# Pairing the first two output chunks of a hybrid attention layer in seven block products, with weight sums made by accumulating transfers

## The reference

```python
h = rmsnorm(x, g_norm)
proj = jnp.einsum('bsd,de->bse', h, w_in)
...
y_moba = rmsnorm(o_moba * jax.nn.silu(m_z), g_out_moba)
...
y_nsa = rmsnorm(o_nsa * jax.nn.silu(n_z), g_out_nsa)
y = jnp.concatenate([y_moba, y_nsa], axis=-1)
return x + jnp.einsum('bse,ed->bsd', y, w_out)     # and then rmsnorm(x, g_final)
```

## Time and profile before

| what | value |
|---|---|
| median of 3 runs | 495.84 us (495.82 to 496.1) |
| the profiled execution | 495.77 us |
| its span, first to last instruction | 494.0 us |
| TensorE busy | 484.8 us (98%), 2502 matmuls |
| VectorE busy | 354.1 us (72%) |
| ScalarE busy | 261.7 us (53%) |
| GpSimd busy | 64.1 us (13%) |
| granted TensorE clock, mean | 0.996 |

### The profile page before, as it was taken

How to read it: one execution, slowest core, us unless ns; L and a number is a source line. 1 busy time by engine, 2 the same in 40 slices (tenths; PEclk the granted TensorE clock), 3 DMA queues, 4 the chain that set the end, 5 groups by cost and what they waited for, 6 DMA issues and landing times.

```text
span 494.0 us, 6523 instructions
## 1 busy us (share of the span) xinstructions
PE 484.8 (98%) x2502; PEld 402.4 (81%) x2502; DVE 354.1 (72%) x561; ACT 261.7 (53%) x374; POOL 64.1 (13%) x66
## 2 busy tenths in 40 slices
PE   8999999999999999999999999999999999999993
PEld 7887787877788888888888888888888888888882
DVE  5888855932699948776587887765888667888643
ACT  5886353642656535645544455664675664366422
POOL 2340100100112202000020200000332240040120
PEclk9999999999999999999999999999999999999998
DMA  8989894577576552543544724448247679433304
GB/s 292 325 287 385 302 330 148 195 251 260 136 268 194 171 171 85 171 130 127 171 142 157 255 63 156 140 151 303 85 148 300 239 266 361 167 139 121 135 0 170
DMA packets 56783, 97.50 MB, mean 197 GB/s; under 512 B 4560, under 2 KB 15408, under 8 KB 56368
## 3 DMA queue, kind: packets, MB, share of 16 engines
q1 hardware_dynamic: 54544, 96.03, 56.7%
q10 hardware_dynamic: 2208, 1.06, 0.9%
HBM read 93.93 MB, written 2.10 MB: 194 GB/s over the span
## 4 chain that ended last, share of the span: by engine, by line
PE 96%; issue 1%; DMA 1%; ACT 0%; DVE 0%; ACTq 0%; POOLq 0%; POOL 0%; SPq 0%; DVEq 0%
PE proj L692 26%; PE proj L694 26%; PE proj L693 26%; PE b_o L988 4%; PE b_t L673 2%; PE b_p L957 2%; PE proj L725 2%; PE b_s L858 2%; PE proj L731 1%; PE proj L736 1%; DMA w_raw<-in_w_in_dram 1%; PE b_s L694 1%; PE b_s L692 1%; PE b_s L693 1%; PE b_p L673 0%
## 5 line engine op out<-in xcount | busy, mean ns | idle before, releaser
L1417 DVE TENSOR_TENSOR w_lo<-w_raw,w_hi 128x2048 fp32r<-128x2048 f32 x65 | 149.6, 2305 | 63.9 <-ACT w_hi L1068 63.8
L692 PE MATMUL proj<-w_hi,xT_hi 128*128 128x512 f32 x490 | 192.9, 394 | 0.0
L694 PE MATMUL proj<-w_hi,xT_lo 128*128 128x512 f32 x490 | 191.1, 390 | 0.0
L693 PE MATMUL proj<-w_lo,xT_hi 128*128 128x512 f32 x490 | 190.9, 390 | 0.0
L1068 ACT ACTIVATE w_hi<-w_raw 128x2048 fp32r<-128x2048 f32 x65 | 124.1, 1912 | 31.6 <-PE proj L694 20.4
L692 PEld LDWEIGHTS proj<-w_hi,xT_hi 128*128 128x128 f32 x490 | 92.0, 188 | 20.3 <-issue 1.6
L694 PEld LDWEIGHTS proj<-w_hi,xT_lo 128*128 128x128 f32 x490 | 92.0, 188 | 19.6
L693 PEld LDWEIGHTS proj<-w_lo,xT_hi 128*128 128x128 f32 x490 | 92.1, 188 | 18.1
L1219 ACT ACTIVATE pT<-b_p 128x512 f32<-128x512 f32 (+2 forms) x24 | 11.7, 489 | 51.6 <-PE b_p L957 51.6
L640 POOL TENSOR_TENSOR rope_a<-rope_a,rope_b 128x512 f32<-128x512 f32 (+1 forms) x12 | 15.0, 1274 | 165.4 <-DVE rope_b L1504 165.4
L1698 DVE TENSOR_TENSOR w_lo<-blk_b,w_hi 128x1024 fp32r<-128x1024 f32 x16 | 19.8, 1236 | 18.3 <-ACT w_hi L1134 18.3
(11 more groups left out here) (261 smaller groups left out, 560.3 us busy)
## 6 DMA issues: line engine op xcount, KB each, us to landing
w_raw<-in_w_in_dram SPq DMA_DIRECT2D x51, 1024.0 KB, 5.1
w_raw<-in_w_out_dram SPq DMA_DIRECT2D x14, 1024.0 KB, 5.2
xo<-in_w_ck_dram SPq DMA_DIRECT2D x4, 1024.0 KB, 8.6
xo<-in_w_cv_dram SPq DMA_DIRECT2D x4, 1024.0 KB, 7.1
w_raw<-in_w_in_dram SPq DMA_DIRECT2D x12, 256.0 KB, 6.8
Q<-in_x_dram SPq DMA_DIRECT2D x1, 2048.0 KB, 10.1
out_dram<-Q SPq DMA_DIRECT2D x8, 256.0 KB, 2.8
xo<-in_x_dram SPq DMA_DIRECT2D x3, 512.0 KB, 7.9
```

Source lines behind the costliest of these rows:

```text
L692: nc.tensor.matmul(dst, a_hi, b_hi, start=first, stop=False, skip_group_check=goes_on)
L693: nc.tensor.matmul(dst, a_hi, b_lo, start=False, stop=False, skip_group_check=goes_on)
L694: return nc.tensor.matmul(dst, a_lo, b_hi, start=False, stop=last, skip_group_check=goes_on)
L1417: nc.vector.tensor_tensor(wl, w_raw[:, u % RAW], wh.bitcast(F32), ALU.subtract).then_inc(lo_ready, 1)
```

## The change

Output chunks 0 and 1 become a pair of the same kind (`OA`, in `PAIRS` between the last z pair and `OUT_PAIR`), done in the two slots 60 and 61 (`oa_first`, `oa_second`) that replace the units (0, 0), (0, 1) and (1, 0); everything after moves up by a slot. The signs of the sums are turned round for both output pairs, so that the weight sums are pure additions. For `OA` they aren't made by VectorE: SyncE loads block B11 three times, B22 twice, B21 once, and GpSimd issues five transfers that add another block of `w_out` into those tiles (`oa_add`). The four intermediate copies of `OA` go to SBUF (with a sign) and are added into `acc` by four more transfers that GpSimd issues. The load of x into `acc` is cut in two, each waiting for blocks of `OA` to have been split. `y_sums`, which fell into slot 60, moves to slot 57, and `ys_residual` from slot 64 to slot 58.

The second part: the last unit's second token half is done in two halves of 256 columns (`last_chunk`), the second into the bank `b_t`, and `last_half` adds and squares them one after the other.

```diff
-OUT_UNITS = [(0, 0), (0, 1), (1, 0), (1, 1), (0, 2), (0, 3), (1, 2), (1, 3)]
+OA_SLOT = NPROJ
+OUT_UNITS = [(1, 1), (0, 2), (0, 3), (1, 2), (1, 3)]
...
 ROUNDED_AT = {9: 10, 10: 11, 11: 12, 12: 13, 13: 14, 14: 15, 15: 16, 17: 17,
-              41: 40, 42: 41, 43: 42, 44: 43, 45: 44, 46: 45, 47: 46, 49: 47, 50: 48, 52: 49, 53: 50, 54: 51, 55: 52, 56: 53, 57: 54, 58: 55,
-              66: 61, 67: 62, 68: 63, 69: 64, 70: 65, 71: 66, 72: 67}
+              41: 40, 42: 41, 43: 42, 44: 43, 45: 44, 46: 45, 47: 46, 49: 47, 50: 48, 52: 49, 53: 50, 54: 51, 55: 52, 56: 53,
+              61: 55, 62: 56, 63: 58, 65: 59, 66: 60, 67: 61, 68: 62, 69: 63, 70: 64, 71: 65}
...
+                if u == 50:
+                    sp.wait_ge(scores_done, len(JOBS))
+                    sp.dma_start(oa_t1, weight_block(OA, "B11")).then_inc(oa_in[1], 16)
+                    sp.dma_start(oa_t2, weight_block(OA, "B11")).then_inc(oa_in[2], 16)
+                if u == 51:
+                    sp.dma_start(oa_t3, weight_block(OA, "B22")).then_inc(oa_in[3], 16)
+                    sp.dma_start(oa_b11, weight_block(OA, "B11")).then_inc(oa_in[0], 16)
+                if u == 53:
+                    sp.wait_ge(blk_sum, 4 * Z2 + 3)
+                    sp.dma_start(oa_b21, weight_block(OA, "B21")).then_inc(oa_in[4], 16)
+                if u == 55:
+                    sp.wait_ge(blk_lo, 7 * OA)
+                    sp.dma_start(oa_b22, weight_block(OA, "B22")).then_inc(oa_in[5], 16)
+                if u == 56:
+                    sp.wait_ge(blk_lo, 7 * OA + 2)
+                    sp.dma_start(acc[:, 0, :], x[0, 0:P, :]).then_inc(acc_in[0], 16)
...
+            def oa_add(n, name, tile):
+                pool.dma_start(tile, weight_block(OA, name), accum_op=ALU.add).then_inc(oa_sum[n], 16)
             for i, kind in enumerate(KINDS[:NC]):
+                if i == 12:
+                    pool.wait_ge(oa_in[1], 16)
+                    oa_add(0, "B12", oa_t1)
+                    pool.wait_ge(oa_in[2], 16)
+                    oa_add(2, "B12", oa_t2)
+                    pool.wait_ge(oa_in[3], 16)
+                    oa_add(1, "B12", oa_t3)
+                if i == 13:
+                    pool.wait_ge(oa_sum[2], 16)
+                    oa_add(3, "B22", oa_t2)
+                if i == 14:
+                    pool.wait_ge(blk_lo, 7 * OA + 4)
+                    oa_add(4, "B21", oa_t2)
...
+            for i in range(4):
+                m, c = ((0, 1), (1, 0), (0, 0), (1, 1))[i]
+                pool.wait_ge(mid_out, 4 * OA + i + 1)
+                pool.wait_ge(acc_in[m], 16)
+                pool.dma_start(acc[:, m, c * CW:(c + 1) * CW], mid_copy(OA, i), accum_op=ALU.add).then_inc(oa_added, 16)
...
+            def oa_first():
+                a, b = PAIRS[OA]
+                bank_free(a)
+                pe.wait_ge(xs_lo_ok, 3)
+                seven(OA, "P1").then_inc(mid_done, 1)
+                seven(OA, "P5").then_inc(unit_used, 1)
+                bank_free(b)
+                seven(OA, "P2")
+                pe.wait_ge(mid_out, 4 * OA + 1)
+                seven(OA, "P6").then_inc(mid_done, 1)
+                pe.wait_ge(mid_out, 4 * OA + 2)
+                pe.wait_ge(ylo_done, 4)
+                unit_rows(UNIT_NO[a, 1], 0).then_inc(unit_used, 1)
+
+            def oa_second():
+                pe.wait_ge(mid_out, 4 * OA + 3)
+                seven(OA, "P7").then_inc(mid_done, 1)
+                seven(OA, "P3")
+                pe.wait_ge(mid_out, 4 * OA + 4)
+                unit_rows(UNIT_NO[PAIRS[OA][0], 1], 1).then_inc(unit_used, 1)
+                seven(OA, "P4").then_inc(unit_used, 1)
...
+                for cols in HALVES:
+                    for k in range(UK):
+                        dst, x_hi_, x_lo_, wh, wl = operands(NU - 1, 1, k)
+                        if cols.start:
+                            last = three_products(b_t[:, 0:CW // 2], x_hi_, x_lo_, wh[:, cols], wl[:, cols], k == 0, k == UK - 1)
+                        else:
+                            last = three_products(dst[:, cols], x_hi_, x_lo_, wh[:, cols], wl[:, cols], False, k == UK - 1, True)
                     last.then_inc(last_done, 1)
...
+                if slot == 57:
+                    block_lo(OA, 0)
+                    block_lo(OA, 1)
+                    y_sums()
+                if slot == 58:
+                    block_lo(OA, 2)
+                    block_lo(OA, 3)
                     ys_residual()
+                if slot == OA_SLOT:
+                    lo(UNIT_NO[NC, 1])
+                    block_lo(OA, 4)
+                    block_lo(OA, 5)
+                if slot == OA_SLOT + 1:
+                    block_lo(OA, 6)
+                    y_scale(1)
```

More of the change, by code:

```diff
@@ L88, in stream @@
                 plain(c, g)
+    ring += [("early", OA), ("middle", OA)]
+    plain(NC, 1)
+    ring.append(("late", OA))
     for c, g in OUT_UNITS[:-1]:
@@ L143, in rounded_at @@
         return slot
-    return slot - 4 if 60 <= slot < 65 else ROUNDED_AT.get(slot)
+    return ROUNDED_AT.get(slot)
 OUT_SLOT = [OUT_DONE[0], OUT_DONE[1] + 1, OUT_DONE[2]]
@@ L771, in seven @@
                 of, k0, m, bank_no, n, new = SEVEN[name]
+                n = OA_BLOCK[name] if p == OA else n
                 pe.wait_ge(blk_lo, 7 * p + n + 1)
-                if of == "s" and p != OUT_PAIR:
+                if of == "s" and p < OA:
                     xh, xl = [t[:, m, k0:k0 + 2, :] for t in (xs_hi, xs_lo)]
                 else:
-                    pair = (ys_hi, ys_lo) if of == "s" else (xT_hi, xT_lo) if p != OUT_PAIR else (ymT_hi, ymT_lo)
+                    pair = (ys_hi, ys_lo) if of == "s" else (xT_hi, xT_lo) if p < OA else (ymT_hi, ymT_lo)
                     xh, xl = [t[:, k0:k0 + 2, m * P:(m + 1) * P] for t in pair]
@@ L1303, in _ @@
                     xs_round((7, 40).index(slot))
-                if slot == 62:
-                    ys_round()
+                if slot == 57:
+                    block_hi(OA, 0)
+                    block_hi(OA, 1)
+                if slot == 58:
+                    block_hi(OA, 2)
+                    block_hi(OA, 3)
+                    ys_round()
+                if slot == 59:
+                    hi(UNIT_NO[NC, 1])
+                if slot == OA_SLOT:
+                    mid_out_(OA, 0)
+                    mid_out_(OA, 1)
+                    block_hi(OA, 4)
+                    mid_out_(OA, 2)
+                    block_hi(OA, 5)
+                    y_squares(3)
+                if slot == OA_SLOT + 1:
+                    mid_out_(OA, 3)
+                    block_hi(OA, 6)
                 for p in range(len(PAIRS)):
@@ L1760, in residual, with last_half @@
                 nc.vector.tensor_tensor(a, proj_b[(NC + c) % 2][m][:, :], a, ALU.add).then_inc(dve_read, 1)
+            def last_half(h):
+                dve.wait_ge(last_done, 2 + h)
+                row = acc[:, 1, 3 * CW:4 * CW]
+                a = row[:, HALVES[h]]
+                if h == 0:
+                    nc.vector.tensor_tensor(row, proj_b[(NC + 3) % 2][1][:, :], row, ALU.add).then_inc(half_added, 1)
+                else:
+                    nc.vector.tensor_tensor(a, b_t[:, 0:CW // 2], a, ALU.add).then_inc(half_added, 1)
+                dve.wait_ge(half_added, h + 1)
+                done = nc.vector.tensor_tensor_reduce(out=rope_a[:, 1, HALVES[h]], in0=a, in1=a, scale=1.0 / D,
+                                                      scalar=ssf[:, 1, 4:5] if h else ssf1[:, 1:2],
+                                                      op0=ALU.mult, op1=ALU.add, accum_out=ssf[:, 1, 3:4] if h else ssf[:, 1, 4:5])
+                done.then_inc(*((ssf_ok, 1) if h else (half_squares, 1)))
             def row_sum(m):
@@ L1770, in final @@
                 a = acc[:, m, 3 * CW:4 * CW]
-                dve.wait_ge(dve_read, dve_reads(NC + 2) + m + 1)
-                nc.vector.tensor_tensor_reduce(out=rope_a[:, m, :], in0=a, in1=a, scale=1.0 / D, scalar=ssf1[:, m:m + 1],
-                                               op0=ALU.mult, op1=ALU.add, accum_out=ssf[:, m, 3:4]).then_inc(ssf_ok, 1)
+                if m == 0:
+                    residual(3, 0)
+                    dve.wait_ge(dve_read, dve_reads(NC + 2) + 1)
+                    nc.vector.tensor_tensor_reduce(out=rope_a[:, m, :], in0=a, in1=a, scale=1.0 / D, scalar=ssf1[:, m:m + 1],
+                                                   op0=ALU.mult, op1=ALU.add, accum_out=ssf[:, m, 3:4]).then_inc(ssf_ok, 1)
+                else:
+                    last_half(0)
+                    dve.wait_ge(half_squares, 1)
+                    last_half(1)
                 dve.wait_ge(rstdf_ok, m + 1)
@@ L1844, in _ @@
                     t2(T2_SLOT.index(slot))
-                if slot == 60:
-                    y_sums()
-                for i, at in enumerate((70, 70, 71, 71)):
+                for i, at in enumerate((69, 69, 70, 70)):
                     if slot == at:
@@ L1896, in _ @@
```

(7 more changed lines are left out.)

128 lines of the change are left out of this document (78 added, 50 removed).

## The result

The changed kernel takes 502.61 us (median of 4 runs, 502.04 to 503.05) against 495.83 us for the kernel before (4 runs beside it): the ratio is 1.0137, with a 95% interval of 1.0124 to 1.0149. It is slower by 6.8 us, where 2.1 was forecast and 500.2 was the upper end of the range. The profiled execution took 502.04 us, its span is 500.2 us, 6.2 more than before. It is the lowest of the four; its mean granted clock is 0.993, that of the other three 0.990 to 0.991.

The account below looks back on a forecast made before the run. TensorE was taken as the bound (96% of the span). Products -1.36, waits +2.9, +0.4 and +0.5, transfers 0 and end -0.36 gave +2.1 us on 495.77, so 497.9 us; for 8 in 10 the range was 495.6 to 500.2 us.

Parts of the forecast that it names:

- The products: TensorE, new slots 60 and 61: 66 matmuls instead of 72, at 0.2268 us each, -1.36 us.
- The first wait: TensorE before P1, the pair's first product, waits for the residual of the sums: +2.9 us, bounds 1.5 and 3.5.
- Transfers: 0, hidden: GpSimd's adding transfers, taken as 5 to 7 us each, hide behind other work: 0 us; the fifth add is tightest.
- Up to the last row of slot 56 nothing has moved: VectorE in front of P1: the old times hold through slot 56, leaving it free at 390.21.
- the granted clock still 1.00: Expected sign in the profile after the change: TensorE's clock stays at 1.00.
- rival (d): The clock falls in TensorE's wait: a few us cost 1 to 2 (499.5), both new slots 7 (505); chance 0.08.
- The second and the third wait: TensorE before units (1, 1) and (0, 3) waits for VectorE's splits: +0.4 and +0.5 us.
- The end: Last unit's second half in two halves: matmuls +0.16, last addition and scan -0.52; sum -0.36 us, bounds 0 and -0.5.
- Rival (c): GpSimd's transfers are late or their descriptors hold up VectorE or GpSimd: about 500 us, up to 508; chance 0.09.
- Rival (a): Before P1 the sums' residual is done by 398.8 and the change is faster: 494.05 us; chance 0.09.
- The range: The forecast's own range, from the bounds of the three waits: +0.1 to +4.8 us, 496.8 to 499.6.
- rival (b): Before P1 only VectorE's own work counts, and the later waits vanish: -0.2, 495.6 us; chance 0.14.

Follow-up runs that it names:

- experiment 2: Changed kernel with GpSimd's third adding transfer, and its wait for the load, moved behind the gating of chunk 12: 500.23 us, ratio 1.0092.
- experiments 1 and 3: 1: changed kernel, 21 unread matmuls in the wait before P1, 500.37 us; 3: 12 such matmuls, third add behind chunk 12's gating, 498.19 us.
- experiment 7: Changed kernel with the third add behind chunk 12's gating and the sums' rounding and residual ahead of blocks 2 and 3: 496.30 us, 1.0010.
- experiments 7 and 9: Experiment 7 has its own line; 9 adds to it P6 ahead of P2 and ScalarE's copy of P1 ahead of silu: 495.83 us, 0.9999.

## Why the prediction was wrong

Its direction was right and its size a third of what came. By its own steps:

- **The products, -1.36**, hold: the sum of the parts closes with them.
- **The first wait, +2.9,** held for what it worked out: with the gating in its old place the wait is 2.85 (experiment 2).
- **"Transfers: 0, hidden"** is the first step that failed, and with it the sentence "Up to the last row of slot 56 nothing has moved", which rests on it. I set the duration of the first adds against GpSimd's idle 15.18 us and took 5 to 7 us for one (they took 5.9 to 9.4). But an add waits for the load of the tile that it adds to: the third tile's load could not be issued before 360.40, and took 11.46 us. The bound was in the rows, since the slowest group of loads of 512 KB has a median of 10.6; from 360.40 that ends at 371.0, 4.3 us behind the gating's start of 366.72. What I left out was the issue time of that load in SyncE's queue. It made P1 2.0 us late (403.74 instead of 401.7).
- **The clock** is the second step that failed: the sum has it at nothing ("the granted clock still 1.00"), and it stood as rival (d), with a chance of 0.08 and a price of 1 to 2 us. It fell behind the waits of 2.85, 3.96 and 4.77 us and did not behind those of 1.03, 1.46 and 1.87. The price was sized about rightly and the chance wrongly: in the order of these waits the clock cost 1.7, 2.6 and 1.7 in the traces, and the medians of experiments 1 and 3 give 2.2 and 2.0 with the 0.2 of P1's quicker start in them. The traces agree with the rule that the prediction cited beside it (the Trainium skill, TensorE: Matmul & The Clock Gate, Part 1), that idle time of the array leads to the lower level. Its upper price, 7 us for both new slots, was too low: 66 matmuls at 0.43 us instead of 0.2268 would cost 13; no run came near it. With a few us of (d) in the sum it would have been about 497.9 + 1.8 = 499.7, still short by the step above.
- **The second and the third wait, +0.4 and +0.5**, are 0.45 and 0.54 in the trace.
- **The end, -0.36**, is -0.30 in the trace and -0.32 as a kernel of its own, whose interval only just excludes none.
- **Rival (c)** spoke of late transfers and named the fifth add as the tightest. The fifth was never late, not even in experiment 7, where ScalarE took block 6 5.6 us earlier (410.08 against 415.67). It was the third. No issue held GpSimd for several us, as the prediction had it as a sign of being wrong.
- **Rival (a)**, the sums in time, is what experiments 7 and 9 make true by the order of the programs. Even then the pair brings nothing: 495.83 with the new end, against 495.50 for the end alone. The six matmuls saved (1.36) are used up by the waits and gaps that are left (1.65): 0.54 in front of (0, 3), some 0.8 at the seven products, which hand over to ScalarE, and small ones.
- **The range:** its lower end, +0.1, takes the end at 0; with the end at -0.36, as the sum has it, the same waits give -0.2, which is rival (b). It changes nothing here, as the miss is at the other end.

The sum: 2.1 forecast, 2.0 (trace) to 2.4 (median of experiment 2) for the late gating, 2.0 to 2.2 (medians of experiments 1 and 3) for the clock make 6.1 to 6.7, against 6.8. How much of experiment 2's further 0.4 is a clock that stays low for a shorter time is open.
